# Narrowing the doubling levels of a chunked recurrence's triangular inverses from 128 to 64 columns

## The reference: what is computed

```python
def step(state, inp):                      # 12 heads of 64 channels, 256 tokens
    r_t, w_t, k_t, v_t, kk_t, a_t = inp
    sa = jnp.einsum('bhvk,bhk->bhv', state, -kk_t)
    state = (state * w_t[:, :, None, :] + sa[..., None] * (kk_t * a_t)[:, :, None, :]
             + v_t[..., None] * k_t[:, :, None, :])
    return state, jnp.einsum('bhvk,bhk->bhv', state, r_t)
```

## Time and profile before

| | |
|---|---|
| median of 3 runs | 2552.52 us (2551.76 to 2553.73) |
| the profiled execution, its own time | 2553.47 us |
| its span, first to last instruction | 2551.7 us |
| PE busy, PEld busy | 92%, 83% |
| DVE busy, ACT busy | 52%, 40% |
| mean granted TensorE clock | 0.952 |
| chain that ended last | PE 85%, DVE 10% |
| the mixer with the inverses | about 370 to 636 us of the span |

### The profile page before, as it was taken

The page is one execution under the profiler, slowest core; times in us unless marked ns, Lnnn a source line. Parts: engine busy times, 40 slices in busy tenths (PEclk is TensorE's granted clock), DMA queues, the critical chain, the costliest instruction groups (busy, mean ns, idle before and its releaser), DMA issues.

```text
span 2551.7 us, 35773 instructions
## 1 busy us (share of the span) xinstructions
PE 2338.2 (92%) x14998; PEld 2112.9 (83%) x14998; DVE 1324.1 (52%) x1675; ACT 1021.4 (40%) x1303; POOL 44.4 (2%) x55
## 2 busy tenths in 40 slices
PE   6899988978878799999998999799998889999887
PEld 6899976867767799999997888698976779898676
DVE  4444645375554555555555455544455554444654
ACT  4333432232443444444443434433444443343542
POOL 0000010010000000000000000000000000000000
PEclk9999986979989899999999999899999999999899
DMA  7456520000643355555554555454540555555033
GB/s 264 148 174 210 186 83 1 1 1 8 231 153 104 125 185 184 182 181 181 181 197 164 187 193 197 151 187 157 198 132 1 164 183 185 178 178 165 1 117 131
DMA packets 217831, 373.12 MB, mean 146 GB/s; under 512 B 8263, under 2 KB 108020, under 8 KB 210804
## 3 DMA queue, kind: packets, MB, share of 16 engines
q1 hardware_dynamic: 211088, 360.48, 42.5%
q10 hardware_dynamic: 6628, 10.98, 1.2%
HBM read 369.32 MB, written 2.12 MB: 146 GB/s over the span
## 4 chain that ended last, share of the span: by engine, by line
PE 85%; DVE 10%; ACT 2%; DMA 1%; issue 1%; POOL 0%; ACTq 0%; DVEq 0%; SPq 0%; POOLq 0%
PE PS L379 25%; PE PS L381 24%; PE PS L380 24%; PE PS L1468 2%; DVE h_lo L592 1%; DVE w_lo L321 1%; PE PS L955 1%; PE PS L1452 1%; DVE small L1505 1%; PE PS L962 1%; DVE spare L1501 1%; PE PS L938 1%; PE PS L1291 1%; PE PS L1290 1%; ACT w_hi L316 1%
## 5 line engine op out<-in xcount | busy, mean ns | idle before, releaser
L321 DVE TENSOR_TENSOR w_lo<-raw,w_hi 128x2048 fp32r<-128x2048 f32 (+2 forms) x340 | 766.4, 2254 | 857.9 <-ACT w_hi L316 855.9
L316 ACT ACTIVATE w_hi<-raw 128x2048 fp32r<-128x2048 f32 (+2 forms) x340 | 640.1, 1883 | 871.3 <-PE PS L381 851.1
L379 PE MATMUL PS<-h_hi,w_hi 128*128 128x256 f32 x2640 | 752.8, 285 | 15.4 <-DVE h_lo L592 11.8
L381 PE MATMUL PS<-h_hi,w_lo 128*128 128x256 f32 x2640 | 751.0, 284 | 0.0
L380 PE MATMUL PS<-h_lo,w_hi 128*128 128x256 f32 x2640 | 751.0, 284 | 0.0
L379 PE MATMUL PS<-w_hi,h_hi 128*128 128x512 f32 (+2 forms) x1440 | 548.1, 381 | 25.4 <-DVE w_lo L321 8.1
L380 PE MATMUL PS<-w_lo,h_hi 128*128 128x512 f32 (+2 forms) x1440 | 545.4, 379 | 0.0
L381 PE MATMUL PS<-w_hi,h_lo 128*128 128x512 f32 (+2 forms) x1440 | 545.1, 379 | 0.0
L379 PEld LDWEIGHTS PS<-h_hi,w_hi 128*128 128x128 f32 x2640 | 510.8, 193 | 17.0 <-DVE h_lo L592 13.1
L380 PEld LDWEIGHTS PS<-h_lo,w_hi 128*128 128x128 f32 x2640 | 510.7, 193 | 0.0
L381 PEld LDWEIGHTS PS<-h_hi,w_lo 128*128 128x128 f32 x2640 | 510.6, 193 | 0.0
(11 more groups left out here) (466 smaller groups left out, 1704.3 us busy)
## 6 DMA issues: line engine op xcount, KB each, us to landing
raw<-in_w_in SPq DMA_DIRECT2D x132, 1024.0 KB, 5.1
raw<-in_ffn_w_up SPq DMA_DIRECT2D x176, 512.0 KB, 4.3
raw<-in_w_out SPq DMA_DIRECT2D x48, 1024.0 KB, 5.1
raw<-in_ffn_w_down SPq DMA_DIRECT2D x44, 1024.0 KB, 4.7
raw<-in_mem_wkv SPq DMA_DIRECT2D x8, 1024.0 KB, 8.2
raw<-in_mem_wq SPq DMA_DIRECT2D x4, 1024.0 KB, 5.2
raw<-in_mem_wo SPq DMA_DIRECT2D x4, 1024.0 KB, 4.9
raw<-in_w_in SPq DMA_DIRECT2D x4, 768.0 KB, 4.5
```

The costliest lines, as they stand in the source:

```text
L316: act.activation(w_hi[:, slot % 2, :st.n], raw[:, slot, :st.n], ACT.Copy).then_inc(hi_made, 1)
L321: dve.tensor_tensor(w_lo[:, slot % 2, :st.n], raw[:, slot, :st.n], w_hi[:, slot % 2, :st.n].bitcast(F32), ALU.subtract).then_inc(lo_made, 1)
L379: pe.matmul(ps, l_hi, r_hi, start=start, stop=False, skip_group_check=skip)
L381: return pe.matmul(ps, l_lo, r_hi, start=False, stop=stop, skip_group_check=skip)
```

## The change

At level l only the columns in the first half of each joined block can get a non-zero entry from the mask: 64 of 128. The new kernel computes, masks and adds these alone. They are packed next to each other in PSUM and in U (view `UL`, 4 matrices of 64 columns); `level_cols` picks them out of X in runs of 2^l columns. At level 6 the product has only 64 rows as well, since U's 64 columns are the weights. The transposes of line 952, their copies to XT, level 0, and everything after the inverses are as before. The number of instructions and their order on every engine are the same.

```diff
+        HALF = P // 2
+        def level_cols(m, l):
+            if len(m.shape) == 2:
+                return m.rearrange("p (b s n) -> p b s n", s=2, n=1 << l)[:, :, 0, :]
+            return m.rearrange("p i (b s n) -> p i b s n", s=2, n=1 << l)[:, :, :, 0, :]
+        def by_blocks(m, l):
+            return m.rearrange("p i (b n) -> p i b n", n=1 << l)
+        def left_mask(l):
+            m = level_cols(level_mask(l), l)
+            return m.unsqueeze(1).to_broadcast([P, 4, HALF >> l, 1 << l])
+        def halves(bank):
+            return PS[:, bank, 0:4 * HALF].rearrange("p (i t) -> p i t", i=4)
...
+            UL = U[:, 0:2, :].rearrange("p a (c t) -> p (a c) t", c=2)
...
-                    last = pe.matmul(psA[:, i, :], mats[:, i, 0, :], X[:, i, :], start=True, stop=True)
+                    last = pe.matmul(halves(A)[:, i, :], mats[:, i, 0, :], level_cols(X[:, i, :], l), start=True, stop=True)
...
-                        last = pe.matmul(psB[:, i, :], XT[:, i, :], U[:, i, :], start=True, stop=True)
+                        last = pe.matmul(halves(B)[:, i, :], XT[:, i, :], UL[:, i, :], start=True, stop=True)
-                        last = pe.matmul(psA[:, i, :], U[:, i, :], XT[:, i, :], start=True, stop=True)
+                        last = pe.matmul(halves(A)[0:HALF, i, :], UL[:, i, :], XT[:, i, HALF:P], start=True, stop=True)
...
-                dve.tensor_tensor(U, psA, bc4(level_mask(l)), ALU.mult).then_inc(j.dve, 1)
+                dve.tensor_tensor(by_blocks(UL, l), by_blocks(halves(A), l), left_mask(l), ALU.mult).then_inc(j.dve, 1)
...
-                    dve.tensor_tensor(X, X, psB, ALU.add).then_inc(j.dve, 1)
+                    dve.tensor_tensor(level_cols(X, l), level_cols(X, l), by_blocks(halves(B), l), ALU.add).then_inc(j.dve, 1)
-                    dve.tensor_tensor(XT, XT, psA, ALU.add).then_inc(j.dve, 1)
+                    dve.tensor_tensor(XT[0:HALF, :, HALF:P], XT[0:HALF, :, HALF:P], halves(A)[0:HALF, :, :], ALU.add)\
+                       .then_inc(j.dve, 1)
```

## The result

Over 12 executions each, the changed kernel takes 2557.61 us (2554.26 to 2562.30) and the kernel before 2553.29 (2551.38 to 2557.65): a ratio of 1.0018 with a 95% interval of 1.001 to 1.0027. So the change costs about 4.3 us, 2.6 to 6.9 by that interval; +2.9 was forecast. The profiled execution lies near the lower end of the twelve, 2554.80 us, 1.3 over the profiled one of before.

What follows compares the result with a forecast made beforehand. PE's stream of weight loads was taken to bound the inverses. Later clock returns (+3.0, +3.7) less line 964 (-2.7) and line 1136 (-1.1) gave +2.9 us: median 2555.4 us, range 2546 to 2584.

Steps and rivals of the forecast that it cites:

- The weights set the pace of lines 955 and 962: Inverse products: 128x128 weight loads, not moving columns, fix 0.111 us per pair at the high clock, 0.213 at the low.
- The term of 0: Lines 955 and 962: halving the moving columns to 64 gains 0 us at unchanged clock.
- Line 964 gains half: Level 6 product: weights shrink to 64 columns, so 2.68 us halves, 1.34 us less per round, -2.7 in all.
- DVE gains nothing but at its few places: Most of DVE's 19.4 us saving lies beside PE; only line 1136 (-1.1) and the second round (-1.6) count.
- The additions of line 1136: Additions to XT of lanes 1 and 2, awaited by line 982: 0.54 us less per round, -1.1 in all.
- The clock comes back later: Both rounds: low clock until about 440 and 580 us, not 433.8 and 567.0; +3.0 and net +3.7; 50%.
- its rule, that streaming counts and not issuing: Streamed columns, not a busy PE queue, bring the high clock back; taken from 375.8 to 386.0 us, at 0.5 throughout.
- the step of the second round: Clock returns after line 1185's 8 full-width matmuls, at 580.3 us; +4.7, less about 1.0 for a covered stall: +3.7.
- Rival 1: Clock returns at 433.8 and 567.0 as before, so gains stand alone: -5.4 us, median 2547.1; 15%.
- Rival 2: Moving columns set the pace: 528 instructions save 29 us, line 964 and the rest 5 more, 2519 us; 4%.
- Rival 3: Clock stays low through second-round levels 2 to 6: +27.7 us there, +30 in all, median 2583; 20% with shorter forms.
- Rival 4: First round misses its return (+30), or clock falls again at PE's waits from line 982 on (+3.4); 11% together.

Runs made afterwards that it cites:

- e4: Changed kernel with line 955 (all levels) and 962 (up to level 5) moving 16 columns, DVE comparing instead of adding; 2617.21 us, 1.0247 of before.
- e8: e3 plus the unread products of e6 ahead of level 1 of lanes 1 and 2; 2550.33 us, 0.9984 of before.
- e6: e2 plus three unread 256-column PE products ahead of level 1 of lanes 1 and 2; 2544.76 us, 0.9965 of before.
- e1: Changed kernel with all PE products back at 128 columns, only DVE narrow; 2552.04 us, 0.9995 of before.
- e3: Changed kernel with level 1 alone back at 128 columns on PE; 2548.33 us, 0.9978 of before.
- e7: Changed kernel plus the unread products of e6 ahead of level 1 of lanes 1 and 2; 2567.46 us, 1.0066 of before.
- e9: e7 with the side lanes' finish issuing its 8 full-width matmuls twice, 16 in a row; 2556.35 us, 1.0004 of before.
- e5: Kernel before with level 6 alone narrowed, matmul and addition to XT; 2551.35 us, 0.9996 of before.
- e2: e1 with level 6 narrow on PE, 64 columns of weights and of moving operand; 2549.06 us, 0.9986 of before.

## Why the prediction was right

*The weights set the pace of lines 955 and 962.* Shown, by e4 most sharply. The term of 0 was slightly off: a row of a lane is 0.05 us shorter with 64 columns, by its first gap. Round 2 in e8 against e6, both without a low clock, is 44.3 to 45.0 us, 0.7 for levels 2 to 6. That is all that 64 fewer columns are worth in 15 lanes' rows of line 955 and 12 of line 962.

*Line 964 gains half.* The forecast was 1.34 us in each round; it measured 1.14.

*DVE gains nothing but at its few places.* In e1 the second round is 1.6 us shorter, as worked out, and the first is not shorter. The additions of line 1136 were put at 0.54 us in each round. Line 982 of lanes 1 and 2 had waited 0.62 us each for them; now these wait 0.37 each for a copy by ACT (line 1067 of the changed kernel), and from line 975 of the first lane to line 982 of the last the time falls by 0.48 and 0.38 us.

*The clock comes back later.* That this comes from the narrow products is shown: they alone stand between e1 and the changed kernel, and those of level 1 alone between e3 and it. In the first round the place was right: the clock returned at 438.3, right behind the side lanes' 12 full-width matmuls and the first lane's transposes, and the round is 1.6 us longer; the steps give +3.0 - 1.3. In the second round it returned at 574.9, ahead of line 1206 (the former 1185), where I had counted on that line and 580.3:

```profile
571.15 1.06 PE L971 MATMUL PS<-ident,side 128*128 128x128 f32 x4
572.00 1.81 PE L974 MATMUL PS<-side 128*128 128x64 f32 x8
573.60 1.06 PE L971 MATMUL PS<-ident,raw_flat 128*128 128x128 f32 x4
574.46 1.20 PE L974 MATMUL PS<-raw_flat,side 128*128 128x64 f32 x8
...
576.78 1.11 PE L1206 MATMUL PS<-raw_flat,arena 128*128 128x128 f32 x8
```

The transposes of two lanes stood to either side of a narrow row. That round is 0.6 us shorter than before, where the steps up to level 6 gave +2.4; the 5.4 us that the clock came back sooner are worth 2.7 at half pace, nearly all of it. The prediction took its rule, that streaming counts and not issuing, from the stretch at 375.8 and called PE as busy there as from 563.5 to 567.0. It was not quite: 92% against 99%, and PEld 81% against 91%; and with line 927's four, 16 of its 38 matmuls move 2 columns, not 12. The rule holds, but it is e4 that shows it.

*The total.* In the profiled execution the step of the second round was therefore 3.0 us too high, and the fall between the rounds, 2.0 us, was only a rival and not a term; over twelve executions the median is 1.4 us above my total. That +2.9 came so near to it is in part luck, for terms that missed in opposite directions stand in the sum. The twelve spread over 8.0 us, and their mean granted clock goes with it: 0.949 and 0.950 in the five shortest, 0.945 in the longest, 2562.30 us. So the spread is the clock's. Where in the other executions it was low stays open, for only one has a trace.

*Rival 1, a clock indifferent to the columns,* is refuted by e1, e3 and e4. *Rival 2, columns setting the pace,* by e4. *Rival 3, low through the second round,* did not come in the changed kernel's trace and did in e7's, with 44 us at 0.5 and a round 16.1 us over before's, where I had worked out +27.7 for a low clock to the end of level 6. What decides isn't settled. In e7 the 8 matmuls of the finish were not enough and in e9 16 were; but transposes with narrow rows between them, which stood where the clock came back in the changed kernel, stood in e7 from 565.2 to 572.6 as well and did not bring it back. *Rival 4* came in part: after, the clock was at 0.5 from 489.5 to 496.4, between the rounds, which the trace of before doesn't show; it cost 2.0 us where the rival had 3.4.

## What to carry to other kernels

Read the pace of small matmuls from their starts, and look for a row with the same weights and far fewer columns: if it is no quicker, fewer moving columns buy nothing, and only fewer or narrower weights do. Then look at what the clock does. A change that removes streamed columns without removing time can keep TensorE at 1.2 GHz for longer, most of all where the engine has just waited. Keep the wide form, or give it something to stream, in the few instructions around such a wait (e3, e6). Narrowing the moving columns of the dense rest as well gained 0.7 us in a round and nothing in the total (e8 against e6); narrowing the weights of level 6 took 1.0 to 1.1 us off each round (e5).

## What the runs showed of the hardware

PE can be busy without a gap for 71.7 us and be granted 1.2 GHz all the time, when most of its matmuls move 16 columns behind 128x128 weights (e4). With 128 columns in the same lines it was granted 2.4 GHz for both whole rounds (e6). Unread matmuls in waits of about 1.5 us were worth more than they cost: 8.2 us under before with them (e6), 3.1 without (e2). Within a row, fp32 pairs of weight load and matmul start 0.111 to 0.112 us apart at the high clock with weights of 128 columns, whether 128, 64 or 16 columns move (before, changed kernel, e4), and 0.058 us apart with weights of 64 columns and 64 moving ones (changed kernel, level 6).
